# Rope keys of the sample requests: one plain load per page instead of sixteen indirect gathers

## The reference, cut to what matters

```
def mla_sample(h, past_lat, past_rope, ...):
    ...                                  # latent keys and rope keys are joined
    o_lat = causal_attention(q, k, k_lat[:, :, None, :], t0)

past_lat = gather_pages(cache_kv_latent[j], page_table)      # (8, 1024, 256)
past_rope = gather_pages(cache_k_rope[j], page_table)        # (8, 1024, 32)
```

## Time and profile before

| | |
|---|---|
| median of 3 runs | 1536.74 us (1536.7 to 1538.36) |
| the profiled execution | 1547.43 us |
| its span from first to last instruction | 1545.7 us |
| PE busy | 1480.5 us (96%) |
| DVE, ACT, POOL busy | 373.4, 258.7, 113.7 us |
| transfers | 463.25 MB, mean 300 GB/s |
| PE's granted clock, mean of the span | 0.985 of full speed |

### The profile page before, as it was taken

The page is one execution under the profiler, slowest core; times in us unless marked ns, Lnnn a source line. Parts: engine busy times, 40 slices in busy tenths (PEclk is TensorE's granted clock), DMA queues, the critical chain, the costliest instruction groups (busy, mean ns, idle before and its releaser), DMA issues.

```text
span 1545.7 us, 24270 instructions
## 1 busy us (share of the span) xinstructions
PE 1480.5 (96%) x9896; PEld 878.8 (57%) x9896; DVE 373.4 (24%) x901; ACT 258.7 (17%) x586; POOL 113.7 (7%) x174
## 2 busy tenths in 40 slices
PE   6999888999999999999998999999999999999997
PEld 2544545788888888778886454543334334423332
DVE  2222532300000065644785100010000200010103
ACT  2222321200000032357604000000000100100001
POOL 1100652000000000010011000000000100010000
PEclk9999989999999999999999999999999999999999
DMA  9858989343334553482389999999999999999995
GB/s 372 329 219 358 365 257 324 121 163 145 129 103 148 192 197 113 140 297 96 116 311 375 366 366 397 390 410 409 418 417 419 404 419 416 419 404 420 417 418 212
DMA packets 100204, 463.25 MB, mean 300 GB/s; under 512 B 12046, under 2 KB 31275, under 8 KB 58453
## 3 DMA queue, kind: packets, MB, share of 16 engines
q1 hardware_dynamic: 86912, 419.46, 69.9%
q0 software_dynamic: 10672, 41.03, 7.8%
q10 hardware_dynamic: 2512, 1.23, 0.3%
HBM read 446.32 MB, written 15.55 MB: 299 GB/s over the span
## 4 chain that ended last, share of the span: by engine, by line
PE 82%; DMA 11%; DVE 3%; issue 1%; SPq 1%; ACT 1%; DVEq 0%
PE bank L1657 11%; PE bank L1175 11%; PE bank L1205 10%; PE bank L1707 5%; PE bank L1219 5%; PE bank L1550 5%; DMA ringx<-in_moe_w_up 4%; PE bank L1268 3%; DMA xT<-in_moe_w_up 3%; PE bank L915 3%; PE bank L1669 3%; PE bank L1565 2%; PE bank L1591 2%; DMA ringx<-in_moe_w_down 2%; DMA ring<-in_w_ada 2%; PE bank L1002 2%
## 5 line engine op out<-in xcount | busy, mean ns | idle before, releaser
L1657 PE MATMUL bank<-ring,hg 128*32 128x512 f32 (+1 forms) x1152 | 158.2, 563 | 5.1 <-DMA ring<-in_moe_w_up 3.0
L1205 PE MATMUL bank<-hT,ring 128*128 128x264 f32 x704 | 156.9, 386 | 0.3 <-ACT hT L1760 0.3
L1205 PEld LDWEIGHTS bank<-hT,ring 128*128 128x128 f32 x704 | 133.7, 190 | 23.4 <-issue 0.6
L1657 PE MATMUL bank<-ringx,hg 128*32 128x512 f32 (+1 forms) x768 | 116.9, 559 | 3.6 <-DMA xT<-in_moe_w_up 2.3
L1175 PE MATMUL bank<-hT,ring 128*128 128x264 f32 x512 | 117.8, 390 | 0.7 <-ACT hT L1760 0.4
L1175 PEld LDWEIGHTS bank<-hT,ring 128*128 128x128 f32 x512 | 97.9, 192 | 18.5 <-issue 1.2
L1657 PEld LDWEIGHTS bank<-ring,hg 128*32 128x32 f32 x1152 | 48.5, 111 | 84.2 <-issue 79.7
L1707 PE MATMUL bank<-ring,turnH 128*32 128x512 f32 x768 | 88.8, 603 | 2.2 <-DMA ring<-in_moe_w_down 2.2
L1219 PE MATMUL bank<-actT,ring 128*128 128x264 f32 x352 | 79.1, 386 | 0.6 <-DVE actT L2258 0.6
L2703 DVE TENSOR_TENSOR actX<-actX,bank 128x512 f32<-128x512 f32 (+1 forms) x18 | 10.8, 640 | 263.4 <-PE bank L1657 263.4
L1219 PEld LDWEIGHTS bank<-actT,ring 128*128 128x128 f32 x352 | 66.8, 190 | 12.4 <-DVE actT L2258 1.0
(11 more groups left out here) (597 smaller groups left out, 1977.6 us busy)
## 6 DMA issues: line engine op xcount, KB each, us to landing
ring<-in_moe_w_down SPq DMA_DIRECT2D x56, 1024.0 KB, 21.5
ring<-in_w_ada SPq DMA_DIRECT2D x48, 1024.0 KB, 10.7
ring<-in_moe_w_gate SPq DMA_DIRECT2D x31, 1024.0 KB, 13.3
ring<-in_moe_w_up SPq DMA_DIRECT2D x28, 1024.0 KB, 18.5
ring<-in_ssm_w_in SPq DMA_DIRECT2D x20, 1024.0 KB, 4.9
ringx<-in_moe_w_up SPq DMA_DIRECT2D x20, 1024.0 KB, 18.3
ringx<-in_moe_w_gate SPq DMA_DIRECT2D x19, 1024.0 KB, 16.7
ringx<-in_moe_w_down SPq DMA_DIRECT2D x13, 1024.0 KB, 20.3
```

What stands on the lines that cost most here:

```text
L1205: m = mm(bank[2 * w + q][:, 0:T], slot8(tl)[:, k, q * P:(q + 1) * P], hT[:, k, :], start=k == 0, stop=k == DC - 1)
L1657: m = mm(bank[2 * b_ + u][rows, 0:HALVES[g][u]], hg[:, k, rows], w[:, kk, 512 * u:512 * u + HALVES[g][u]], start=k == 0, stop=k == DC - 1, ...
```

## The change

The gathers, the table broadcasts and the DVE instruction go, with the constant column they used. A new function `load_rope` loads one page of one sample: 32 rows of 128 values, 16 KB, a plain transfer. POOL loads the 32 rope pages of samples 0 to 3, SP those of samples 4 to 7, each sample's behind its turned pages and a wait on the queries; SP's count on the ring slot's semaphore, so that PE's wait for the slot covers them. POOL no longer holds 40 page numbers: `page_ids` is called anew for the eight of a sample before each batch of loads (turned, rope and token pages).

```
+    def load_rope(eng, ids_, b, n):
+        rows = slice(32 * (b % 4), 32 * (b % 4) + 32)
+        return eng.dma_start(rope_page(b // 4, n)[rows, :], a["cache_k_rope"][ds(ids_[b][n], 1), :, :].rearrange("a r t -> (a r) t"))
...
@@ SP
                 load_turned(sp, sample_pages, b, n).then_inc(ring_ready[(LAT + b - 4) % NS], 16)
+            sp.wait_ge(s["q_ready"], H)
+            for n in range(NPG):
+                load_rope(sp, sample_pages, b, n).then_inc(ring_ready[(LAT + b - 4) % NS], 16)
...
@@ POOL
-        for j in range(4):
-            g.dma_start(pages_all[32 * j:32 * j + 32, :, :], ...).then_inc(s["rope_in"], 16)
...
-        sample_pages = page_ids(g, (0, 1, 2, 3, 7))
 
         def turned(b):
+            sample_pages = page_ids(g, (b,))
             for n in range(NPG):
                 load_turned(g, sample_pages, b, n).then_inc(keys_in[b], 16)
 
         def tokens(b):
+            sample_pages = page_ids(g, (b,))
             for n in range(NPG):
                 load_tokens(g, sample_pages, b, n).then_inc(lat_ready[b], 16)
-
-        def rope_keys(g_):
-            for n in range(NPG):
-                g.indirect_dma_start(out=rope_page(g_, n), ...).then_inc(s["rope_in"], 16)
...
         g.wait_ge(s["q_ready"], H)
-        rope_keys(0)
-        g.wait_ge(s["rope_in"], 64 + 16 * NPG)
-        rope_keys(1)
+        for b in range(4):
+            sample_pages = page_ids(g, (b,))
+            for n in range(NPG):
+                load_rope(g, sample_pages, b, n).then_inc(s["rope_in"], 16)
...
@@ PE
-            pe.wait_ge(s["rope_in"], 16 * (4 + NPG * (g_ + 1)))
+            if g_ == 0:
+                pe.wait_ge(s["rope_in"], 16 * 4 * NPG)
...
@@ DVE
-        v.wait_ge(s["rope_in"], 64)
-        v.tensor_scalar(rope_rows[:], pages_all[:], float(ROPE), cst[:, C_ROW:C_ROW + 1], ALU.mult, ALU.add)
```

More of the change, by code:

```diff
@@ L154, in moe_value @@
     slot = (t % MS + WOUT) % NS
-    before = len(range(slot, MOE, NS)) + (NPG - 1 if slot in LAT_SLOTS else 0) if t % MS < NS else NPG if t % MS >= NS + EXTRA else 0
+    before = len(range(slot, MOE, NS)) + (2 * NPG - 1 if slot in LAT_SLOTS else 0) if t % MS < NS else NPG if t % MS >= NS + EXTRA else 0
     return 16 * (before + t // MS + 1)
@@ L184 @@
 C_SPARE = C_HALF + 1
-C_ROW = C_SPARE + 2
-C_MOST = C_ROW + 1
+C_MOST = C_SPARE + 2
 C_NEED = C_MOST + 4 * NE
@@ L207, in ready_value @@
 def ready_value(n):
-    return 16 * (n // NS + 1) + (16 * (NPG - 1) if n >= LAT and n % NS in LAT_SLOTS else 0)
+    return 16 * (n // NS + 1) + (16 * (2 * NPG - 1) if n >= LAT and n % NS in LAT_SLOTS else 0)
 def build(nc, a, o):
@@ L270, in build @@
     qpeT = sb("qpeT", [P, 2, 32], c=c1)
-    pages_all = sb("pages_all", [P, 2, NPG], I32, c=c1)
-    rope_rows = sb("rope_rows", [P, 2, NPG], I32, c=c1)
     olatT = sb("olatT", [P, KC, NB, H], c=c1)
@@ L726, in _ @@
         g.dma_start(wqb, a["mla_w_qb"][0].rearrange("(c p) n -> p c n", p=P)).then_inc(s["pool_in"], 16)
-        for j in range(4):
-            g.dma_start(pages_all[32 * j:32 * j + 32, :, :], a["page_table"].rearrange("(u j) n -> j u n", j=4)[j].unsqueeze(0).to_broadcast(
-                [32, 2, NPG])).then_inc(s["rope_in"], 16)
         g.memset(qpeT[:, :, H:32], 0.0).then_inc(s["zeroed"], 1)
         g.memset(qlatT[:, :, :, H:32], 0.0).then_inc(s["zeroed"], 1)
-        sample_pages = page_ids(g, (0, 1, 2, 3, 7))
         def turned(b):
+            sample_pages = page_ids(g, (b,))
             for n in range(NPG):
@@ L739, in tokens @@
         def tokens(b):
+            sample_pages = page_ids(g, (b,))
             for n in range(NPG):
                 load_tokens(g, sample_pages, b, n).then_inc(lat_ready[b], 16)
-        def rope_keys(g_):
-            for n in range(NPG):
-                g.indirect_dma_start(out=rope_page(g_, n), out_offset=None, in_=a["cache_k_rope"].rearrange("a r t -> (a r) t"),
-                                     in_offset=bass.IndirectOffsetOnAxis(ap=rope_rows[:, g_, n:n + 1], axis=0)).then_inc(s["rope_in"], 16)
         turned(2)
@@ L2770, in constants @@
     c[:, C_SPARE] = T + 1 + i
-    c[:, C_ROW] = i % ROPE
     c[:, C_SPARE + 1] = 2 * (T + 1) + i - i // CAPL
```

## The result

The changed kernel took a median of 1574.6 us (1574.03 to 1575.21) against 1537.55 for the kernel before on the same chip: a ratio of 1.0225, interval 1.0208 to 1.0242. It is slower, as forecast, but by 37 us and not by 12.9, and 25 us above the predicted 1549.6. On two other chips the changed kernel, unaltered, gave 1.0207 and 1.0204 (29.4 and 30.2 us). The profiled execution took 1574.39 us, its span 1572.8.

What follows compares the result with a forecast made beforehand. PE was 82% of the chain; POOL's 102.8 us of sequencing from 151.9 would delay L1137 from 253.6 to 266.5, +12.9. Profiled 1547.43 plus 12.9 is 1560.3, less 10.7 gives 1549.6 us; range 1543 to 1556.5, slower 0.87.

Steps and rivals of the forecast that it cites:

- last page of sample 7 starts: POOL's last DMA for sample 7: predicted at 260.9, 6.2 us after that sample's first page is sequenced at 254.7.
- L1137 resumes: PE continues L1137 once sample 7's pages have landed: 266.5 instead of 253.6, +12.9 us added to the end.
- L1205 starts: PE's 704 multiplies, at 301.47 before: predicted to start near 314, with their 157 us unchanged.
- SP's 64 loads less before's 32 (29.18): SP's queue: 32 added rope pages at 0.49 us each add 15.7 us, so SP ends at 238.2 instead of 222.5.
- POOL's sequencer: From 151.9, 12 id batches (53.8 us) plus turned, rope and token pages sum to 102.8 us before sample 7's first page.
- SP's part: Rival where SP's late token pages set the end: +3.3 us, 1540.0; chance 0.08. The main forecast has them hidden behind 266.5.
- PE's stalls: PE's issue stalls in L1047, L1037 and L1038, up to 5.5 us, counted zero; rival gets them back, 1531.2, chance 0.06.
- A third of the 10.7: Term of the range's lower end: 3.4 us less if ids and landings are quicker without the profiler.
- The median of the runs shown is 1536.74, 10.7 lower, and I carry that over: Profiled 1547.43 us plus 12.9 gives 1560.3; taking off the profile's 10.7 over the median gives 1549.6.
- the landing, 5.6 us: Sample 7's last page, started at 260.9, lands after 5.6 us, the median of these pages before, at 266.5.
- a rival, with 8.5 us: Small transfers land late: 8.5 us landings, shift 18.4 us, 1555; forecast together with late landings has chance 0.86.
- a slack of 12.2: SP's 12.2 us wait for the scores before its 24 loads, taken as room for its added rope pages.

Runs made afterwards that it cites:

- e2_ids_again: The kernel before, gathers kept, with page ids read again before each batch of POOL's turned and token pages: 1557.65 us, ratio 1.0093.
- e4_pool_part: The kernel before with group 0's rope keys by 32 plain POOL loads, group 1's gathers without the landing wait, ids read in two goes: 1549.0 us, ratio 1.0008.
- e13_sp_between: The changed kernel with only SP's 32 rope pages moved ahead, to where SP waits for the ring: 1571.15 us, ratio 1.0198.
- e0_before: The kernel before, unaltered, run for a second trace: 1541.62 us, ratio 0.9999, span 1537.7.
- e3_hold_weights: The changed kernel with SP waiting for sample 7's pages before loading dense-layer weights: 1566.14 us, ratio 1.0156.
- e13_after: The changed kernel, unaltered, run on one chip with e13_sp_between: 1573.35 us, ratio 1.0204.
- e8_shared: The kernel before with sample 7's turned pages loaded by POOL instead of SP and no wait for the gathers' landing: 1552.22 us, ratio 1.0037.
- e5_sp_part: The kernel before with only SP's turned and rope pages as in the change; POOL gathers group 0, reads ids once: 1556.61 us, ratio 1.0065.
- e1_ids_early: The changed kernel with page ids read in two goes, before the turned and before the token pages, 72 reads instead of 104: 1558.04 us, ratio 1.0097.
- e9b_rope_between: e1_ids_early with SP's rope pages moved ahead of its turned pages, between the last eight ADA1 tiles: 1549.81 us, ratio 1.0023.

## Why the prediction was wrong in size

The steps, set against the trace after:

| step | predicted | trace after |
|---|---|---|
| last page of sample 7 starts | 260.9 | 261.46 |
| its landing | 5.6 | 12.39 |
| L1137 resumes | 266.5 | 273.89 |
| L1205 starts | 314.4 | 327.38 |
| SP's 64 loads end | 238.2 | 234.3 |
| SP's 64 loads less before's 32 (29.18) | 15.7 | 15.8 |
| last rope page on POOL | 215.0 | 214.5 |

**Right.** The main step, POOL's sequencer: ids aren't read beside its DMA steps, and 102.8 us of them from 151.9 put the last start within 0.6 us. That the miss is so small is in part luck: the first id is read at 150.2 and not at 151.9, the sequence up to sample 7's first page takes 105.5 us and not 102.8 (rope and token pages cost 0.56 to 0.58 us each), and the last start follows 5.8 us later and not 6.2. e2_ids_again shows that reading the ids again is enough for a slowdown of 14 to 16 us, e4_pool_part that the rope loads on POOL cost nothing, e13_sp_between that SP's part is hidden. Counting zero for PE's stalls was right too: in the changed kernel PE was through with the prompt's heads at 212 and then waited 4.3 us for the rope pages of group 0. SP's rope pages were sized right as well (45.0 us for 64 loads, 189.24 to 234.26). A third of the 10.7 is 3.6 and not 3.4, which hardly moves the range.

**Wrong: the step "The median of the runs shown is 1536.74, 10.7 lower, and I carry that over", with +12.9 counted from 253.6.** Of the 25.0 us between 1549.6 and 1574.6 it is the largest term. The profiled execution of before was late by 9.2 us at L1137 (253.60 against 244.42 in e0_before), and that lateness arose after 152, where the changed kernel's POOL has its last wait behind it. There the resume time hangs on POOL's start at 150 to 152, so the lateness isn't there to be subtracted: the changed kernel's profiled time, 1574.39, stands 0.2 from its median. Of the 10.7, the spans place 8.0 (1545.7 against 1537.7); the other 2.7 lie between e0_before's execution and the first median (1539.38 against 1536.74) and were not placed. Counted from 244.4, the predicted 266.5 was already +22.1.

**Wrong: the landing, 5.6 us.** It was taken from pages that SP's weights hadn't reached, and as the median of all eight where the last one counts (the last two took 6.7 us before). In the changed kernel the weights are issued from 247.8, ahead of sample 7's pages, and those take 12.39: 6.8 us more. The prediction had this as a rival, with 8.5 us, a row from a stretch under the weight stream; with eight tiles of 1 MB just issued it took longer. e3_hold_weights shows the cause.

**Missing: PE's clock after a wait.** From the resume to L1205 it is 53.5 us after, 47.9 in before's trace and 49.2 in e0_before: 5.6 and 4.3 us. The rows of the chain show it: L1137's 58 multiplies take 6.40 instead of the 3.65 for 60 of the earlier trace rows, L1156 3.63 instead of 2.08; the granted clock is 0.50 from 274 to 278, right after PE's wait. The prediction took all that follows the resume as unchanged. In e13_after, where L1156 takes 2.08 again, the whole shift from e0_before is 30.1 us at L1137 (274.50 - 244.42) and 30.2 in the span (1567.9 - 1537.7). That execution is the shortest of its five, though, and by the medians the clock isn't what sets the first chip's 37 us apart from the 30 of e13_after: the changed kernel is only 1.3 us slower there (1574.6 against 1573.35), the kernel before 5.6 us faster (1537.55 against 1543.18).

The account against the forecast's 1549.6: 10.7 not to be carried over; landing 6.8 and start 0.6; clock 5.6; 1.2 behind L1205; 0.2 between profile and median: 25.1 of 25.0 (each rounded).

**Right for the wrong reason.** SP's part was put at 3.3 us if it stood alone, from a slack of 12.2 that only the late execution had; measured alone it is 9.6. Behind POOL's this made no difference.

**Open.** Runs of the kernel before scatter from 1535 to 1556 us over the chips, those of the changed kernel from 1569 to 1576, so its cost is known as 29 to 37 us and no closer. Where before's first execution lost its time can be read, though. Between 170 and 204 the profile shows DVE and ACT waiting for something that it can't name ("remote"), the longest ahead of

```profile
203.65 0.42 DVE L2179 TENSOR_REDUCE mx<-bank 128x1 f32<-128x256 f32 x1 [9.76 <-remote]
```

Such stalls stand in four of the six traces of kernels that gather (before, e8_shared, e4_pool_part, e5_sp_part; the longest 5.7 to 14.3 us), each time while gathers are being issued or within about 3 us of the last, and in none of the ten traces of kernels without gathers. In e0_before and e2_ids_again, which gather as well, there are none. So the gathers are the suspect for before's late execution and perhaps for its scatter, but nothing here shows how, and no run was made to test it.

## What to carry to other kernels

Before a delay is added to a profile's time, ask where in the trace that execution was late: a chain on another engine that starts earlier and waits for nobody doesn't inherit the lateness, so count its end against a second, undisturbed execution. Loop-invariant scalar reads belong where their engine waits anyway, since its sequencer does nothing else meanwhile. When a small load slips behind a weight stream, take its landing from pages that were issued behind as many megabytes, and allow for multiplies at half clock behind a long new wait of PE, as behind the 17.5 us of e1_ids_early.

## What the runs showed of the hardware

Reading one page number into a register, with the check of its range, costs POOL's sequencer 0.55 us (eight in 4.4), as much as issuing a 16 KB load (0.49 in e4_pool_part, 0.56 in the changed kernel). Sample 7's eight pages of 128 KB took a median of 8.6 us to land with eight tiles of 1 MB issued just ahead of them (the last page 12.39), and 5.7 with four. And SP's 32 loads of 16 KB between tiles of 1 MB took a median of 15.5 us to land in e9b_rope_between (24 of the 32; the others 16.4) and drew the tiles' own landing from 12.4 us (e0_before) to 17.4.
